# Choice of experts and places of rows: from VectorE to GpSimd

## The reference, cut to what matters

```python
def moe_swiglu(h, router, w_gate, w_up, w_down):
    probs = jax.nn.softmax((h @ router).astype(jnp.float32), axis=-1)
    top_p, top_i = lax.top_k(probs, TOP_K)
    top_p = top_p / jnp.sum(top_p, axis=-1, keepdims=True)
    combine = jnp.sum(jax.nn.one_hot(top_i, N_EXPERTS) * top_p[..., None], axis=-2)
    ...
    hid = jax.nn.silu(a) * u * combine[..., None]
    return jnp.einsum('bsef,efd->bsd', hid, w_down)
```

## Time and profile before

| | |
|---|---|
| Time, median of 3 runs (lowest to highest) | 1925.7 us (1922.33 to 1929.22) |
| The profiled execution: its time, its span | 1921.34 us, 1919.5 us |
| Mean granted TensorE clock | 0.971 |
| Busy, share of the span: PE, PEld, DVE, ACT, POOL | 93%, 78%, 52%, 41%, 13% |
| Chain that ended last: PE, ACT, DVE, DMA, SP's queue, issue | 81%, 5%, 5%, 5%, 2%, 2% |

### The profile page before, as it was taken

How to read it: one execution, slowest core, us unless ns; L and a number is a source line. 1 busy time by engine, 2 the same in 40 slices (tenths; PEclk the granted TensorE clock), 3 DMA queues, 4 the chain that set the end, 5 groups by cost and what they waited for, 6 DMA issues and landing times.

```text
span 1919.5 us, 32369 instructions
## 1 busy us (share of the span) xinstructions
PE 1785.3 (93%) x14036; PEld 1503.8 (78%) x14036; DVE 1002.3 (52%) x1290; ACT 787.2 (41%) x1094; POOL 257.6 (13%) x221
## 2 busy tenths in 40 slices
PE   5999899999989999998998999999988799899994
PEld 3888688887869999877997788888867356468884
DVE  2866345444745443337963445546448044257885
ACT  3345622234344222224365422325345143347774
POOL 2610033231000000005300223320002000000001
PEclk9999899999999999998999999999999999899997
DMA  9652052216552344337521412226458978959994
GB/s 350 221 196 94 1 210 67 89 46 209 176 197 71 126 131 131 132 135 259 209 88 50 165 64 93 89 89 219 172 212 297 376 253 287 373 191 335 374 381 146
DMA packets 186387, 350.74 MB, mean 183 GB/s; under 512 B 5097, under 2 KB 60417, under 8 KB 185744
## 3 DMA queue, kind: packets, MB, share of 16 engines
q1 hardware_dynamic: 182464, 335.01, 49.5%
q0 software_dynamic: 3792, 13.80, 2.0%
HBM read 319.43 MB, written 29.36 MB: 182 GB/s over the span
## 4 chain that ended last, share of the span: by engine, by line
PE 81%; ACT 5%; DVE 5%; DMA 5%; SPq 2%; issue 2%; POOL 0%; POOLq 0%; DVEq 0%; ACTq 0%
PE bank L1100 6%; PE bank L1671 5%; PE bank L1102 5%; PE bank L1101 5%; PE bank L1640 5%; PE bank L1641 5%; PE bank L1643 5%; PE bank L1528 3%; PE bank L1526 3%; PE bank L1527 3%; PE bank L1136 3%; PE bank L1138 3%; PE bank L1137 3%; PE bank L1341 2%; PE bank L1478 2%
## 5 line engine op out<-in xcount | busy, mean ns | idle before, releaser
L1102 PE MATMUL bank<-hT_hi,ring_split 128*128 128x384 f32 x576 | 196.1, 340 | 0.0
L1777 ACT ACTIVATE ring_split<-ring 128x1024 fp32r<-128x1024 f32 (+2 forms) x84 | 119.5, 1440 | 180.1 <-DMA ring<-in_ffn_w_up 102.5
L2635 DVE TENSOR_TENSOR ring_split<-ring,ring_split 128x2048 fp32r<-128x2048 f32 (+1 forms) x28 | 73.9, 2670 | 142.7 <-ACT ring_split L1777 142.7
L1100 PE MATMUL bank<-hT_hi,ring_split 128*128 128x384 f32 x384 | 142.4, 371 | 4.3 <-DVE modv L2306 2.9
L721 DVE TENSOR_TENSOR ring_split<-ring,w_upper_a 128x1536 fp32r<-128x1536 f32 (+2 forms) x54 | 96.5, 1814 | 76.9 <-PE bank L1671 68.7
L1138 PE MATMUL bank<-ring_split,hT_hi 128*128 128x256 f32 x480 | 135.6, 283 | 0.0
L1101 PE MATMUL bank<-hT_lo,ring_split 128*128 128x384 f32 x384 | 130.9, 341 | 0.0
L1671 PE MATMUL bank<-ring,hT 128*64 128x256 f32 (+1 forms) x592 | 110.4, 513 | 17.6 <-DMA ring<-in_moe_w_up 14.0
L1528 PE MATMUL bank<-hT_hi,ring_split 128*128 128x384 f32 x352 | 118.8, 337 | 0.0
L1526 PE MATMUL bank<-hT_hi,ring_split 128*128 128x384 f32 x352 | 117.6, 334 | 0.0
L1527 PE MATMUL bank<-hT_lo,ring_split 128*128 128x384 f32 x352 | 117.2, 333 | 0.0
(11 more groups left out here) (427 smaller groups left out, 4406.1 us busy)
## 6 DMA issues: line engine op xcount, KB each, us to landing
ring<-in_w_in SPq DMA_DIRECT2D x28, 2048.0 KB, 9.0
ring<-in_ada_w SPq DMA_DIRECT2D x24, 2048.0 KB, 13.0
ring<-in_moe_w_gate SPq DMA_DIRECT2D x32, 1024.0 KB, 8.1
ring<-in_moe_w_up SPq DMA_DIRECT2D x32, 1024.0 KB, 10.3
ring<-in_moe_w_down SPq DMA_DIRECT2D x16, 1536.0 KB, 9.1
ring<-in_w_branch SPq DMA_DIRECT2D x8, 1536.0 KB, 12.4
ring<-in_ffn_w_gate SPq DMA_DIRECT2D x11, 1024.0 KB, 5.4
ring<-in_ffn_w_up SPq DMA_DIRECT2D x11, 1024.0 KB, 7.9
```

The source lines that it names most:

```text
L1100: mm(out, hi, hT_hi[:, k], start=k == 0, stop=False)
L1102: last = mm(out, lo, hT_hi[:, k], start=False, stop=k == KT - 1)
```

## The change

`choose_items` and `place_rows` leave VectorE's queue and go to GpSimd's, ahead of its waits for the scatter. They start when `route_ok` is 4, which is when `rank`, `cnt` and `esel` are there; `cnt` is now copied before `esel`. VectorE keeps `cnt` and the three instructions of the combine weights (`weights`). Where GpSimd's form of an instruction differs: a comparison of two tensors is a subtraction and a comparison with 0, a `scalar_tensor_tensor` is two instructions, and a reduction over 8 is three additions (`sum_of_8`). So 41 instructions of VectorE (27 in `choose_items`, 14 in `place_rows` without the three of the weights) become 64 of GpSimd (42 and 22).

```diff
@@ block.gpsimd, behind the load of route @@
+            g = nc.gpsimd
+            sel, ranked = sel2
+            def sum_of_8(out, x):
+                n = len(x.shape) - 1
+                parts = (slice(None),) * n
+                link(g.tensor_tensor(x[parts + (slice(0, 4),)], x[parts + (slice(0, 4),)], x[parts + (slice(4, 8),)], ALU.add))
+                link(g.tensor_tensor(x[parts + (slice(0, 2),)], x[parts + (slice(0, 2),)], x[parts + (slice(2, 4),)], ALU.add))
+                return g.tensor_tensor(out, x[parts + (0,)], x[parts + (1,)], ALU.add)
+            def choose_items():
+                link(g.tensor_scalar(key, cnt, float(NE), None, ALU.mult))
+                link(g.tensor_tensor(key, key, iota8, ALU.subtract))
+                link(g.tensor_scalar(key[:, 0:1], key[:, 0:1], float(2 * NE * TOK), None, ALU.add))
+                link(g.tensor_tensor(tri8, key.unsqueeze(1).to_broadcast([P, NE, NE]), bc(key, NE), ALU.subtract))
+                link(g.tensor_scalar(tri8, tri8, 0.0, None, ALU.is_gt))
+                link(sum_of_8(nrank, tri8))
+                ...
+                for a in range(4):
+                    last = g.tensor_tensor(looked[:, :, a], tri8, by_rank[:, a].unsqueeze(1).to_broadcast([P, NE, NE]), ALU.mult)
+                link(last)
+                link(sum_of_8(given, looked))
+                ...
+                link(g.tensor_tensor(own, lo, bc(item, NE), ALU.subtract))
+                g.tensor_scalar(own, own, 0.0, None, ALU.is_le)
+                ...
+                g.tensor_scalar(table[:, NI + 1:NI + 2], e_hi[:, NE - 1:NE], 1.0, None, ALU.subtract).then_inc(route_ok, 1)
+            def place_rows():
+                ...
+                for j, pk in enumerate(picks):
+                    last = sum_of_8(place2[:, :, j], pk)
+                link(last)
+                g.tensor_copy(row_of, place2.rearrange("p t j -> p (t j)")).then_inc(route_ok, 1)
+            pool.wait_ge(route_in, 16)
+            pool.wait_ge(route_ok, 4)
+            choose_items()
+            place_rows()
             pool.wait_ge(zero_out, 16 * DEPTH)
             pool.wait_ge(ht_ev, 2 * NT)
             pool.wait_ge(route_ok, 6)
@@ block.vector @@
                     link(v.tensor_tensor(rank, v3(B[6][:, 32:56], NT), sel, ALU.mult))
+                    link(v.tensor_copy(cnt, B[6][:, 56:64]))
                     v.tensor_tensor(esel, slot1.unsqueeze(1).to_broadcast([P, NT, SLOTS]), bc(rank[:, :, 0], SLOTS),
                                     ALU.is_equal).then_inc(route_ok, 1)
-                    link(v.tensor_copy(cnt, B[6][:, 56:64]))
-                    def choose_items():
-                        ...
-                    def place_rows():
+                    def weights():
                         dve.wait_ge(rl_e, 1)
                         link(v.tensor_scalar(m8[:, 0::8], m8[:, 1::8], 1.0, None, ALU.add))
                         link(v.reciprocal(m8[:, 0::8], m8[:, 0::8]))
-                        link(v.tensor_tensor(m8[:, 1::8], m8[:, 1::8], m8[:, 0::8], ALU.mult))
-                        ...
+                        v.tensor_tensor(m8[:, 1::8], m8[:, 1::8], m8[:, 0::8], ALU.mult)
@@ the order at the end @@
                     lower(1, 0)
-                    choose_items()
-                    place_rows()
+                    weights()
```

More of the change, by code:

```diff
@@ L371, in build @@
         own, own2, own3 = (v3(kk(NI * NE), NI) for _ in range(3))
-        key, nrank, over, to_rest = (kk(NE) for _ in range(4))
+        key, nrank, over, to_rest, spare = (kk(NE) for _ in range(5))
         given = v3(kk(NE * 4), NE)
@@ new lines, in place_rows @@
+            def place_rows():
+                link(g.tensor_scalar(to_rest, e_lo, float(SLOTS), None, ALU.mult))
+                link(g.tensor_tensor(to_rest, to_rest, given[:, :, 2], ALU.subtract))
+                link(g.tensor_scalar(to_rest, to_rest, -1.0, None, ALU.add))
+                link(g.tensor_tensor(to_rest, to_rest, given[:, :, 1], ALU.subtract))
+                link(g.tensor_tensor(to_rest, to_rest, given[:, :, 3], ALU.subtract))
+                at, first, room, jump, rest = (x.unsqueeze(1).to_broadcast([P, NT, NE])
+                                               for x in (*(given[:, :, a] for a in range(4)), to_rest))
+                link(g.tensor_tensor(ranked, rank, first, ALU.add))
+                link(g.tensor_scalar(past, rank, float(SLOTS), None, ALU.is_gt))
+                link(g.tensor_tensor(past, past, jump, ALU.mult))
+                link(g.tensor_tensor(ranked, ranked, past, ALU.add))
+                link(g.tensor_tensor(past, rank, room, ALU.subtract))
+                link(g.tensor_scalar(past, past, 0.0, None, ALU.is_gt))
+                link(g.tensor_tensor(past, past, rest, ALU.mult))
+                link(g.tensor_tensor(ranked, ranked, past, ALU.add))
+                for pk in picks:
+                    last = g.tensor_tensor(pk, pk, ranked, ALU.mult)
+                link(last)
+                for j, pk in enumerate(picks):
+                    last = sum_of_8(place2[:, :, j], pk)
+                link(last)
+                g.tensor_copy(row_of, place2.rearrange("p t j -> p (t j)")).then_inc(route_ok, 1)
@@ L2749, in place_rows @@
                         link(v.reciprocal(m8[:, 0::8], m8[:, 0::8]))
-                        link(v.tensor_tensor(m8[:, 1::8], m8[:, 1::8], m8[:, 0::8], ALU.mult))
[L2751 to L2760, removed]
-                        link(v.tensor_tensor(ranked, ranked, past, ALU.add))
-                        for pk in picks:
-                            last = v.tensor_tensor(pk, pk, ranked, ALU.mult)
-                        link(last)
-                        for j, pk in enumerate(picks):
-                            last = v.tensor_reduce(place2[:, :, j], pk, AX.X, ALU.add)
-                        link(last)
-                        v.tensor_copy(row_of, place2.rearrange("p t j -> p (t j)")).then_inc(route_ok, 1)
+                        v.tensor_tensor(m8[:, 1::8], m8[:, 1::8], m8[:, 0::8], ALU.mult)
                     def lower(j, i, s=None):
```

21 lines of the change are left out of this document (added).

## The result

The changed kernel takes 1947.06 us (median of 6 runs, 1938.57 to 1948.6), the kernel before, on the same chip, 1926.61 us (6 runs, 1922.33 to 1930.29). The ratio is 1.009, 95% interval 1.0067 to 1.0112: some 20 us slower by the medians, 13 to 22 us by the interval. The profiled execution took 1947.21 us, with a span of 1945.2 us and a mean granted clock of 0.963.

What follows compares the result with a forecast made beforehand. Up to 1534 the end was taken to hang on SyncE's release by the scatter, hence on when `row_of` is ready. Places +22.9, scatter -3.1 gave +19.8, the stall's 9.4 being waited away: 1945 us, range 1930 to 1957.

Steps and rivals of the forecast that it cites:

- VectorE without the routing: Unit 2's first subtraction starts at 1438.8 instead of 1447.49; TensorE's 7.46 us stall before unit 2 of visit 0 goes.
- the 9.4 us: TensorE's gain by the end of unit 5: 7.5 us of stall plus 1.9 us at the lower clock behind it.
- GpSimd's work by itself: The 64 moved instructions on GpSimd, ahead of the scatter: 20.0 us, bounds 14.5 and 30.3.
- The lock: GpSimd works only while line 721 is not running on VectorE; `row_of` ready at 1470.5 against 1447.6, 22.9 us later.
- The rivals without a lock or with a loose one: GpSimd runs through beside line 721: 1920, chance 0.13; it gets more done between subtractions: 1932, chance 0.15.
- the one with dear instructions: Rival: GpSimd's 64 small instructions take 30.3 us of work, time 1956; chance 0.15.
- The scatter: GpSimd's six scatter issues, with VectorE out of work, take 10.0 us, 3.1 us shorter; bounds no gain and 5.1.
- SyncE's release: SyncE's queue, waiting for the scatter, is let go at 1483.9 instead of 1464.05: 22.9 - 3.1 = +19.8 us.
- TensorE's stall: TensorE stands still some 25 us for side 0's rows, landing at 1487.5 and wanted at 1462.8.
- That the end moves by as much as the release: The full DMA stretch up to 1534 starts 19.8 us later with the same bytes; its end moves by the same.
- The sum: +19.8 us on the profiled 1921.34 is 1941.1; on the median 1945.5, said as 1945.
- a scatter that gains nothing: If making descriptors is left free by `tensor_tensor`, the scatter gains nothing and 22.9 us stand.

Runs made afterwards that it cites:

- hold: The changed kernel, but VectorE starts no subtraction of visit 0 before GpSimd has made the rows' places; 1931.45 us, ratio to before 1.0022.
- late_scatter: The kernel before, routing still on VectorE, with 68 linked GpSimd memsets that no result needs put ahead of the scatter; 1944.6 us, ratio 1.0087.
- Experiments 1 and 5: 1: changed kernel, VectorE's subtractions held until GpSimd is through, 1931.45 us; 5: kernel before, routing early on VectorE, in part 1918.55 us, whole 1919.09 us.
- early_split: The kernel before, ranking and places moved ahead of visit 0's first subtraction on VectorE, table and weights left behind unit 1; 1918.55 us, ratio 0.9942.
- experiments 1 and 4: 1: changed kernel, VectorE's subtractions held back, 1931.45 us; 4: kernel before plus linked GpSimd memsets, copies, tensor_scalar and tensor_tensor ahead of the scatter, 1940.03 us.

## Why the prediction was right, and where its sizes were off

- **VectorE without the routing: right.** The 7.46 us are gone. In the row of the stretch below (columns as in the earlier trace rows) the granted clock is 1.00, where the earlier trace rows have 0.81, so the clock's part of the 9.4 us came too (it falls later instead, behind the wait of 20.9 us). The same row shows GpSimd busy for 29.09 of 30.40 us with 21 entries, most of it waiting.

```profile
1442.20:1472.60 30.40, 30.25 (x146) 26.27 (x147) 29.55 (x22) 19.74 (x15) 29.09 (x21) 1.00 0.31 104
```

- **GpSimd's work by itself: right, a little low.** 20.0 us forecast, 21.6 measured in hold.
- **The lock: right in kind, in place and nearly in size.** The account said that GpSimd is held up until line 721 ends (t0 + 42.0) and then needs 7.4 us. It ended at t0 + 40.0, and the rest took 6.4: places ready at t0 + 46.5 instead of t0 + 49.4. The 2.9 us are the first term that was too large: VectorE was done 2.0 us sooner than I reckoned, and 1.0 us less work was left. I had counted 1.6 us for the instructions that GpSimd slips in. From unit 2 on VectorE's busy time grew by only 0.8 us (from 21.14 to 21.91), and its waits for ScalarE shrank from 2.2 to 0.8 us. The rivals without a lock or with a loose one are refuted by hold beside the changed kernel, and the one with dear instructions by hold alone (21.6 us, not 30.3).
- **The scatter: right in sign, too small.** I took 3.1 us, from the shortest issue of 1.36 us, with 5.1 as the far bound. Issues took 0.95 to 1.13 us, and the release came 11.0 us behind the first instead of 15.6: 4.5 us.
- **SyncE's release: +15.5 in the first pair of traces, +15.4 in the means, against +19.8.** The two terms above, 2.9 and 1.4, are all of the difference.
- **TensorE's stall: 20.9 us, against some 25.** Smaller by the same 4 us.
- **That the end moves by as much as the release: right.** +15.5 of end for +15.4 of release, and late_scatter gives the same with another cause. Experiments 1 and 5 show where that rule ends: in hold the release has not moved and the end is 4.7 us later, and in early_split -16 of release is worth -10.9. In both SyncE waits for TensorE's buffers and hardly for the scatter (3.6 and 4.8 us).
- **The sum.** The forecast of 1945 us lies 2 us from the median, but that closeness is luck, by offsetting: +19.8 was forecast for the stretch, where it is +15.5, and some 6 us came from t0, of which the forecast said nothing.

The Trainium skill's "SBUF — State Buffer", section "Who interferes with whom", says that a `tensor_tensor` with both inputs in SBUF contends with GpSimd's reads; experiments 1 and 4 agree (7.96 against 30.41 us, and the copy's 1.71 against 0.24). Its inference that the making of descriptors is left free by `tensor_tensor` looks at first as if it failed: issues take 1.36 to 2.49 us beside line 721 and 0.95 to 1.13 behind it. The rows of the kernel before say where that time goes:

```profile
1454.70 2.28 DVE L721 TENSOR_TENSOR ring_split<-ring,w_upper_b 128x2048 fp32r<-128x2048 f32 x1
...
1455.32 2.49 POOL L1010 DMA_INDIRECT xslots<-hT,ktok  x1 [0.30 <-issue]
...
1456.90 1.75 DVE L721 TENSOR_TENSOR oT_split<-oT,w_upper_a 128x1536 fp32r<-128x1536 f32 x1
```

The issue that begins at 1455.32 ends at 1457.81, 0.83 us behind the end of the subtraction at whose side it began (1456.98), while the next subtraction runs. All six issues of this trace end 0.83 to 0.96 us behind such an end, five of them while the next one runs. In late_scatter an issue that begins with a subtraction, at 1476.20, takes 1.04 us beside it. An issue thus waits once, at its start, for the subtraction that runs, and what follows is not slowed by the next one, which agrees with the inference. The issue has `row_of` in SBUF as an input (`ktok` in the rows); that the wait is for reading it is argued and not shown. What does not hold is the prediction's step from the inference to a scatter that gains nothing: it gained 4.5 us, for the waits at the start of the issues went.

## What to carry to other kernels

Before small work is moved from VectorE to GpSimd, look at what VectorE runs meanwhile: beside a row of large subtractions with both inputs in SBUF, a small instruction that reads SBUF mostly waits until one of them is over (13 of the 21 entries from 1442.2 to 1472.6 us took over 1 us), and 21.6 us of work took 45.8. A stall of TensorE on the moved work is not the price of that work; ask which queue its result lets go, here SyncE's with the weight loads behind it. Where the result is short work that opens a queue, do it first, even on the busy engine: 9 us of routing ahead of the subtractions delayed TensorE by 3 us at the visit's start (a wait of 5.2 us, 2.1 before) and let SyncE go 13 us sooner.

## What the hardware showed that was not expected

- Memsets on GpSimd are not held up by VectorE's subtraction: 0.25 us each for 180 elements, 68 of them, and 0.15 us for 64.
- One-input forms are: a copy of 64 elements 1.71 us against 0.24, tensor_scalar 2.29 against 0.38.
- Issues of the indirect DMA are lengthened beside the subtraction as well, to 2.2 to 2.5 us at the most against 0.95, by one wait at their start. They were cheap in late_scatter too (0.96 to 1.32) once VectorE was nearly through.
- VectorE and GpSimd thus hold each other up with no semaphore between them. GpSimd slips in its small instructions between and into VectorE's others at little cost to VectorE: line 721's members of 2048 elements took 2.48 us at most, against 2.28.
